# A hybrid decoder layer on one core: the mixing stage reordered, with the scan branch ahead of the attention

## What is computed

```
z = rmsnorm(x, g_mix) @ w_in
q, k, v, lru_x, lru_g, sc_b, sc_c, sc_u = split(z)
a = sliding_window_attention(q, k, v, sinks)          # window 128, 8 query heads, 2 KV heads
xc = causal_conv4(lru_x) + bias
r, i = sigmoid(xc @ wa + ba), sigmoid(xc @ wi + bi)   # block-diagonal, 4 blocks of 64
h = scan(exp(-8 r softplus(-lam)), sqrt(1 - a^2) * i * xc)
b = h * gelu(lru_g)
c = sc_b * causal_conv3(sc_c * sc_u)
x = x + concat(rmsnorm(a), rmsnorm(b), rmsnorm(c)) @ w_out
u, g = split(causal_conv3(rmsnorm(x, g_ffn) @ w_up))
x = x + (silu(g) * u) @ w_down
y = rmsnorm(x, g_final)
```

## Time and profile before

| | |
|---|---|
| runs | 1273.22, 1272.29, 1272.14 us |
| profiled execution | 1271.69 us, its span 1269.6 us |
| PE busy | 1173.3 us, 92% |
| DVE, ACT, POOL busy | 796.7, 337.4, 85.1 us |
| mean granted clock of TensorE | 0.963 |
| chain that ended last | PE 84%, DVE 9%, ACT 3%, POOL 1%, issue 1% |

### The profile page before, as it was taken

One profiled execution on the slowest core, in us unless ns is written; L12 is line 12 of the kernel. 1 busy time (PEld: TensorE's weight loads), 2 busy tenths in 40 slices (PEclk: granted clock), 3 DMA queues, 4 the chain that ended last, 5 costly groups with the idle time before them and its releaser, 6 DMA issues.

```text
span 1269.6 us, 18130 instructions
## 1 busy us (share of the span) xinstructions
PE 1173.3 (92%) x6972; PEld 1117.2 (88%) x6972; DVE 796.7 (63%) x1489; ACT 337.4 (27%) x512; POOL 85.1 (7%) x54
## 2 busy tenths in 40 slices
PE   7898899997587878999999999999999999999976
PEld 7897667677477878999999999999999999999965
DVE  6416456849765456756666666666666766666657
ACT  7112375544244233211111111111121211111132
POOL 0311000011023430000000000000000000000000
PEclk9998799999779888999999999999999999999988
DMA  6220000010323321111111111111111011111003
GB/s 221 88 78 21 17 17 17 17 35 34 119 100 100 116 92 59 34 52 48 50 50 49 34 50 50 50 33 50 49 50 50 33 50 50 50 50 42 24 14 134
DMA packets 25174, 72.11 MB, mean 57 GB/s; under 512 B 3472, under 2 KB 10000, under 8 KB 25104
## 3 DMA queue, kind: packets, MB, share of 16 engines
q1 hardware_dynamic: 21984, 64.44, 15.0%
q10 hardware_dynamic: 3152, 7.15, 1.6%
HBM read 66.76 MB, written 5.87 MB: 57 GB/s over the span
## 4 chain that ended last, share of the span: by engine, by line
PE 84%; DVE 9%; ACT 3%; POOL 1%; issue 1%; ACTq 0%; DMA 0%; DVEq 0%; SPq 0%
PE psum L1214 68%; PE psum L1371 6%; PE psum L1323 2%; PE psum L1246 2%; PE psum L1277 2%; POOL w_lo L385 1%; PE psum L1415 1%; PE psum L1333 1%; PE psum L1259 1%; ACT h_hi L1437 1%; ACT w_hi L424 1%; DVE zb L837 1%; PE psum L1269 1%; DVE att L818 1%; DVE zb L953 1%
## 5 line engine op out<-in xcount | busy, mean ns | idle before, releaser
L1214 PE MATMUL psum<-h_hi,w_hi 128*128 128x344 f32 x1392 | 455.3, 327 | 4.4 <-POOL w_lo L385 4.4
L1214 PE MATMUL psum<-h_lo,w_hi 128*128 128x344 f32 x1392 | 449.0, 323 | 0.0
L1214 PE MATMUL psum<-h_hi,w_lo 128*128 128x344 f32 x1392 | 448.7, 322 | 0.0
L1214 PEld LDWEIGHTS psum<-h_hi,w_hi 128*128 128x128 f32 x1392 | 265.4, 191 | 11.3 <-issue 5.7
L1214 PEld LDWEIGHTS psum<-h_lo,w_hi 128*128 128x128 f32 x1392 | 265.3, 191 | 1.4 <-issue 0.5
L1214 PEld LDWEIGHTS psum<-h_hi,w_lo 128*128 128x128 f32 x1392 | 265.4, 191 | 0.0
L424 ACT ACTIVATE w_hi<-raw 128x1024 fp32r<-128x1024 f32 x106 | 111.7, 1057 | 494.9 <-PE psum L1214 456.3
L1214 PE MATMUL psum<-act_hi,w_hi 128*128 128x344 f32 x528 | 175.1, 332 | 0.0
L1085 DVE TENSOR_TENSOR x_sb<-psum,x_sb 128x344 f32<-128x344 f32 x240 | 122.0, 515 | 83.6 <-PE psum L1214 83.6
L1214 PE MATMUL psum<-act_hi,w_lo 128*128 128x344 f32 x528 | 170.1, 322 | 0.0
L1214 PE MATMUL psum<-act_lo,w_hi 128*128 128x344 f32 x528 | 169.3, 321 | 0.0
(11 more groups left out here) (193 smaller groups left out, 1188.8 us busy)
## 6 DMA issues: line engine op xcount, KB each, us to landing
raw<-in_w SPq DMA_DIRECT2D x106, 512.0 KB, 3.2
x_sb<-in_x ACTq DMA_DIRECT2D x8, 516.0 KB, 5.0
out_y<-x_sb SPq DMA_DIRECT2D x12, 344.0 KB, 2.4
x_sb<-in_x SPq DMA_DIRECT2D x2, 1376.0 KB, 11.4
x_sb<-in_x SPq DMA_DIRECT2D x4, 344.0 KB, 5.4
zb<-in_ck ACTq DMA_DIRECT2D x1, 512.0 KB, 3.8
zb<-in_cv ACTq DMA_DIRECT2D x1, 512.0 KB, 4.5
out_k_old<-in_k_keep ACTq DMA_DIRECT2D x1, 508.0 KB, 4.8
```

The costliest lines, as they stand in the source:

```text
L1214: ins = mm(out, a, b, start=(at == 0), stop=(at == n - 1))
```

## The change

The slots are loaded in another order: k, lru_x, lru_g, lru_x, lru_g, v, q (4), sc_c, sc_u, sc_c, sc_u, sc_b, sc_b. The first 30 jobs (slots 0 to 9) run without attention, and under them the whole scan branch: convolutions, gates (three matmuls in a row into three banks), sigmoids, decays, scan, and the B norm.

The 16 attention steps then hold the 12 jobs of sc_c and sc_u, six chunks of 3 matmuls to a step, three before the tasks and three behind (`fill`). The six jobs of sc_b follow, two in the last two steps. Their eviction multiplies by the convolution, which was scaled by the norm before. The A norm of tile 0 is taken within the steps. The norms A and C of tiles 1 and 2, the scalings and splits of these tiles stand under output jobs 0 to 13, the split and squares of the new x by one or two blocks under jobs 8 and 14 to 23. The feed-forward part begins with six jobs (two slots, tile by tile, six PSUM banks), each waiting block by block for the split of x; the third tile is split under them. The issues of the small transfers go from ACT to SP, with the reload of x. The DVE twin of `x2_hi`, `x2_lo`, makes `h_lo` of each block and adds its squares to one sum.

```diff
+K_SLOT, LX_SLOTS, LG_SLOTS, V_SLOT, Q_SLOT0, SC_SLOTS, SU_SLOTS, SB_SLOT0 = 0, (1, 3), (2, 4), 5, 6, (10, 12), (11, 13), 14
+Z_BLOCK = (0, 6, 7, 8, 9, 1, 2, 3, 4, 5, 10, 11, 13, 14, 12, 15)
...
+FILL_JOB0 = NT * SC_SLOTS[0]
+SB_JOB0 = NT * SB_SLOT0
...
+FILLS = NT * 4 * KD // UNITS
+FILL_END = {(KD * (n + 1) - 1) // FILLS: n for n in range(NT * 4)}
+X2_AT = {8: (0, 0, 1), 14: (0, 1, 3), 15: (0, 3, 5), 16: (0, 5, 7), 17: (0, 7, 8), 18: (1, 0, 2), 20: (1, 2, 4), 21: (1, 4, 6),
+         22: (1, 6, 7), 23: (1, 7, 8)}
...
+    for t, j in enumerate((3, 5, 6)):
+        put(j, ("norm", "x", t), "A")
+    put(20, ("v", 0), "V")
...
+        put(25 + t, ("norm", "B", t), "A")
+    for i in range(UNITS + 2):
+        if i >= 2:
+            put(("step", i), ("pv", i - 2), "V")
+        if i < 4:
+            put(("step", i), ("sample", i), "V")
+        if i == 10:
+            put(("step", i), ("norm", "A", 0), "A")
+    put(SB_JOB0 + 2, ("norm", "C", 0), "A")
+    for o, name in ((1, "A1"), (3, "C1"), (8, "A2"), (10, "C2"), (18, "X0")):
+        put(OUT_JOB0 + o, ("norm", name[0], int(name[1])), "A")
+    put(FFN_JOB0, ("norm", "X", 1), "A")
+    put(FFN_JOB0 + 3, ("norm", "X", 2), "A")
...
+                if s == 4:
+                    sp.wait_ge(gate_zeroed, 1)
...
+                if s == 9:
+                    sp.wait_ge(job_read, NT * (V_SLOT + 1))
...
+                if s == 10:
+                    sp.wait_ge(b_ready, 2)
...
+                if s == OUT_SLOT0 + 2:
+                    sp.wait_ge(scratch_free, 1)
...
             root(("norm", "x", 1), rstd[:, tile(1)], D)
+            hi(3)
             root(("norm", "x", 2), rstd[:, tile(2)], D)
...
+            hi(4)
+            sigmoids(0, 0)
+            hi(5)
+            sigmoids(0, 1)
+            decays(0)
+            lru_sqrt(0)
+            gelu(0)
+            hi(6)
+            hi(7)
+            sigmoids(1, 0)
+            sigmoids(1, 1)
+            decays(1)
+            lru_sqrt(1)
+            hi(8)
+            gelu(1)
+            act.wait_ge(b_ready, 2)
+            square(zb[:, 6:8, :], sq_b)
+            hi(9)
+            for t in range(NT):
+                root(("norm", "B", t), rstd_b[:, tile(t)], 2 * P)
+            hi(10)
...
+                if i % 4 == 0:
+                    hi(11 + i // 4)
+                if i == 8:
+                    act.wait_ge(att_ready, 6)
+                    square(q_sb[:, :, tile(0)], sq_a0)
...
+            def x2_hi(t, k0, k1):
+                if k0 == 0:
+                    act.wait_ge(job_done, OUT_JOB0 + KD * (t + 1))
+                    if t:
+                        act.wait_ge(task_done, done_at(("norm", "X", t - 1)))
+                for k in range(k0, k1):
+                    act.wait_ge(job_read, OUT_JOB0 + KD * t + k + 1)
+                    nc.scalar.activation(h_hi[:, k, tile(t)], x_sb[:, k, tile(t)], ACT.Copy,
+                                         scale=gain_ffn[:, k:k + 1]).then_inc(x2_hi_ready, 1)
+                    if k > 2:
+                        act.wait_ge(x2_added, (KD - 1) * t + k - 2)
+                    nc.scalar.activation(x2_sq[k % 2] if k else x2_sum, x_sb[:, k, tile(t)],
+                                         ACT.Square).then_inc(x2_sq_ready, 1)
...
             merged_ab(0)
+            square_c(0)
+            root(("norm", "C", 0), rstd_c[0], 2 * P)
             merged_c(0)
+            hi(OUT_SLOT0)
+            for o in range(NT * KD):
+                hi(OUT_SLOT0 + o + 1)
+                if o in (0, 6):
+                    square_a(1 + o // 6)
+                if o in (1, 7):
+                    square_c(1 + o // 6)
+                if o in (1, 8):
+                    root(("norm", "A", 1 + o // 8), rstd_a[1 + o // 8], HG * P)
+                if o in (3, 10):
+                    root(("norm", "C", 1 + o // 10), rstd_c[1 + o // 10], 2 * P)
+                if o in (4, 11):
+                    merged_ab(1 + o // 11)
+                if o in (5, 12):
+                    merged_c(1 + o // 12)
+                if o in X2_AT:
+                    x2_hi(*X2_AT[o])
+                if o == 18:
+                    root(("norm", "X", 0), rstd[:, tile(0)], D)
+            hi(FFN_SLOT0 + 1)
+            root(("norm", "X", 1), rstd[:, tile(1)], D)
+            x2_hi(2, 0, KD)
+            root(("norm", "X", 2), rstd[:, tile(2)], D)
...
+                if s in LX_SLOTS:
                     if t == 0:
+                        dve.wait_ge(xc_ready, 1)
                         V.memset(x_pad[:, 0:3], 0.0)
                     evac(j, x_pad[:, 3:], samples(x_pad, 4)[:, :, 3])
...
+                elif s in LG_SLOTS:
+                    evac(j, g_in[LG_SLOTS.index(s)])
+                elif s == V_SLOT:
+                    evac(j, vT)
+                else:
+                    evac(j, q_sb[:, s - Q_SLOT0, :])
+                if j in (7, 15):
+                    conv_lru((j - 7) // 8)
+                if j in (12, 19):
+                    gate_input((j - 12) // 7)
+                if j in (13, 20):
+                    lru_root((j - 13) // 7)
+                if j in (14, 21):
+                    lru_scan((j - 14) // 7)
...
+            for i in range(UNITS + 2):
+                if 1 <= i <= UNITS:
+                    rescale(i - 1)
+                if i < UNITS:
+                    score_max(i)
+                if i == 8:
+                    sc_conv(0)
+                if i == UNITS:
+                    sc_conv(1)
+                if i >= 2:
                     att_evac(i - 2)
...
+                if i < 4:
+                    sample_task(i)
+                if i in FILL_END:
+                    fill_evac(FILL_END[i])
+                if i == 9:
+                    sq_tree("A", 0, HG, sq_a0)
+                if i == 12:
+                    a_scale(0)
+                if i >= UNITS:
+                    sb_evac(i - UNITS)
...
+            for o in range(NT * KD):
+                if o + 1 < NT * KD:
+                    w_lo2(OUT_SLOT0 + o + 1)
                 else:
                     dve.wait_ge(w_lo_ready, FFN_SLOT0)
                     w_lo_ffn(FFN_SLOT0)
...
+                out_evac(o)
+                if o in (0, 7):
+                    sq_tree("A", 1 + o // 7, HG, sq_a)
+                if o in (2, 9):
+                    a_scale(1 + o // 9)
+                    sq_tree("C", 1 + o // 9, 2, sq_c)
+                if o in (4, 11):
+                    c_scale(1 + o // 11)
+                if o in (5, 6, 12, 13):
+                    t, k0 = 1 + o // 12, 3 * (o in (6, 13))
+                    ab_lo(t, k0, k0 + 3)
+                    if k0:
+                        c_lo(t)
+                if o in X2_AT:
+                    x2_lo(*X2_AT[o])
+                if o == 19:
+                    reciprocal(("norm", "X", 0), rstd[:, tile(0)])
+            w_lo_ffn(FFN_SLOT0 + 1)
...
-            w_lo_ffn(FFN_SLOT0 + 1)
+            x2_lo(2, 0, KD)
+            reciprocal(("norm", "X", 1), rstd[:, tile(1)])
             carry_in(0, pad_g)
-            ffn_evac(FFN_JOB0, 0, pad_g, None)
-            ffn_evac(FFN_JOB0 + 1, 1, pad_g, None)
-            reciprocal(("norm", "X", 2), rstd[:, tile(2)])
-            ffn_evac(FFN_JOB0 + 2, 2, pad_g, None)
+            carry_in(1, pad_u)
+            for f in range(len(FIRST_JOBS)):
+                s, t = FIRST_JOBS[f]
+                if f == 4:
+                    reciprocal(("norm", "X", 2), rstd[:, tile(2)])
+                ffn_evac(FFN_JOB0 + f, t, (pad_g, pad_u)[s], None, first_ps[f])
             gate_half(0)
             w_lo_ffn(FFN_SLOT0 + 2)
-            carry_in(1, pad_u)
-            for t in range(NT):
-                ffn_evac(FFN_JOB0 + 3 + t, t, pad_u, None)
+            dve.wait_ge(conv_g_ready, 1)
             up_half(0)
...
+            def fill(i, lo, hi):
+                for chunk in range(FILLS * i + lo, FILLS * i + hi):
+                    n, k = divmod(chunk, KD)
+                    j = FILL_JOB0 + n
+                    s, t = z_job(j)
+                    if k == 0:
+                        w_lo_wait(s, None)
+                        pe.wait_ge(job_read, j - 2)
+                    wh, wl = wslot(s, k)
+                    mm(job_ps[j % 3], wh, h_hi[:, k, tile(t)], start=(k == 0), stop=False)
+                    mm(job_ps[j % 3], wh, h_lo[:, k, tile(t)], start=False, stop=False)
+                    ins = mm(job_ps[j % 3], wl, h_hi[:, k, tile(t)], start=False, stop=(k == KD - 1))
+                    if k == KD - 1:
+                        ins.then_inc(job_done, 1)
...
+            for j in range(FILL_JOB0):
+                if j < len(FIRST_JOBS):
+                    first_job(j, 0, h_ready).then_inc(job_done, 1)
+                else:
+                    job(j, *z_job(j)).then_inc(job_done, 1)
+                if j in (10, 11, 17, 18):
+                    gates(j // 16, (10, 11, 17, 18).index(j) % 2)
+                if j == 20:
```

(28 more changed lines are left out.)

540 lines of the change are left out of this document (235 added, 305 removed).

## The result

Measured together on one chip, the changed kernel takes 1213.01 us (median of four runs, 1211.76 to 1214.87) and the kernel before 1272.22: a ratio of 0.9539, 95% interval 0.9528 to 0.9551. The forecast was 1203, in a range of 1190 to 1222.

The account below looks back on a forecast made before the run. PE was taken as the bound, with gains only from its waits and slow matmuls before 508.4 us. Stretches summed to 439.5 + 761.2 = 1200.7, plus 2.1 around: 1203 on the median's scale, range 1190 to 1222.

Parts of the forecast that it names:

- First 30 jobs: Start to attention: 21 jobs after 46.8 us, plus gates, norms and transposes; ACT's work at nothing; attention from 137 us.
- held by ACT or the scan: Rival, first 30 jobs: six weight slots each 1.5 us late, late scan stops jobs; 12 more, 1215; chance 0.15.
- Attention steps: 16 steps: 8.0 us each in steps 4 to 15, 38.8 for steps 0 to 3, 3.4 exposed on DVE; 138.2 us.
- Last two steps and B jobs: Between attention steps and output projection: six jobs, two products, transposes, a norm and a weight wait; 28 us.
- Output projection: 24 jobs 90.5 us, five norms 2.9, queue waits 5.9, POOL and DVE interference 5.4; 104.7 us in all.
- The term for POOL and DVE: Output jobs from 14 on: POOL halves delay DVE, jobs take 4.3 to 4.4 us, 0.6 shows nine times; 5.4 us.
- The queue waits: Output projection: PE's bare waits from ACT's and DVE's queues, for a norm, held-up weights and a root; 5.9 us.
- Entry of the feed-forward part: First six feed-forward jobs: 5.5 us wait for DVE's weight 2 split, 1.6 for slow matmuls; 31 us, nothing gained.
- output part becomes DVE's: Rival, output projection: late jobs also wait for ACT's squares and POOL, 5.5 us each; 18 more, 1221; chance 0.17.
- slower: Rival, attention steps: overlap of two units lost, 12.8 us a step in series; 77 more, 1280; chance 0.02.
- no effect: Rival, whole kernel: the waits of PE come back elsewhere one for one; chance 0.01.
- Nearly all waits go: Rival: no 5.5 us feed-forward stall, steps at PE's bare 7.84, half the output waits gone; 1189; chance 0.12.

Follow-up runs that it names:

- number 3: Changed kernel with the second channel's gate matmuls put after jobs 18 and 19 instead of 17 and 18 on PE: 1207.51 us.
- number 9: Changed kernel with feed-forward weight 2's split and the attention root earlier, second gates later, and ACT's weight 3 split behind the third input-norm root: 1191.96 us.
- number 7: Kernel before with only ACT's split of weight 3 moved ahead of the third root of the input norm: 1265.11 us, ratio 0.9950.
- number 4: Changed kernel with POOL's part of each output weight split cut from 512 to 8 columns, the rest not computed: 1207.88 us.
- number 1: Changed kernel with DVE's split of feed-forward weight 2 moved from behind the gate convolution to behind the fifth eviction: 1206.62 us.

## Why the forecast held, and where its 10 us went

- **First 30 jobs, 6.8 us short of the 137.6 that the terms add up to: the step that failed.** I had worked out what POOL and DVE cost each other for the late output jobs alone, and put it at nothing in the first 30 jobs. I had put "1.5 us late" on the second convolution and nothing on ACT and the input norm. The wait for the convolution is 4.2 us, 2.7 more, and by the rows above two DVE instructions held by POOL's splits account for all 4.2 (2.30 us for 0.14 and 2.31 for 0.23), so that the order behind the scan alone would have cost nothing; number 3 covers this wait and does not test its cause. Its gates and the job behind it run slowly, about 1.7 (2.29 and 4.96 us from start to start, against 1.48 and 4.04). The job ahead of the input norm of tile 2 waits 0.4 for an eviction, and that norm 1.4, which is POOL's split of weight 3 beside DVE's addition (0.52 us of work, 2.57 long). That is 6.2 of 6.8. With numbers 3 and 9 applied the attention starts at 137.35. The bare count (21 jobs, 15 single matmuls, transposes) was right and the cover of the rest was not: the earlier weight 3, which I had costed as pure gain (number 7: 5.9 of 6.2), moved a POOL instruction beside one of DVE's. ACT's long block, which the rival "held by ACT or the scan" rested on, cost nothing; its other half, a late DVE stopping the gates in PE's queue, came true with about half of its 12 us.
- **Attention steps, 1.9 short, out of two errors.** Quiet steps take 7.88 us (8.0), steps 0 to 3 36.4 (38.8), the convolution and the norm's additions 2.0 (3.4): 5.2 us better. One step then takes 15.2 instead of 7.9, for the root. I had asked what DVE and ACT have in a step by durations, not where in ACT's queue the root stands and which PSUM tile it holds.
- **Last two steps and B jobs:** 28.6 for 28.
- **Output projection:** 104.8 for 104.7. The agreement to 0.1 us is partly luck. The late jobs take 4.25 us on the mean, but this holds a norm (0.6) and a wait of 1.4 for POOL's half, which the forecast counted apart or not at all; without them it is 4.05, not 4.3 to 4.4. The term for POOL and DVE was 5.4, all of it in the late jobs; number 4 measures 3.6 there and 1.4 before them, 4.9 together. The queue waits (5.9) are what number 4 leaves above the jobs and norms: 99.9 - 93.4 = 6.5. The two errors cancel. The mechanism was right: a split takes 0.57 us alone and 1.62 beside a POOL half. The rule of the Trainium skill (SBUF — State Buffer, "Who interferes with whom"), on which the prediction drew, is borne out for these DVE instructions. One row was misread: the POOL half of 1.31 us in the earlier trace rows does not lie alone, it starts 0.3 us into four DVE splits, which take 2.89 us.
- **Entry of the feed-forward part:** 29.6 and a slow job behind it, 2.4 in the rest; I had 31 with 1.6 for the slow job in it, so 32.0 against 31. "Nothing gained" there was right, and number 1 shows the reason.
- **Rest:** 761.2 as soon as that wait is gone. A slip of reading that nothing hangs on: the lowest clock in the earlier trace rows is 0.89, not 0.88.
- The rivals "output part becomes DVE's", "slower" and "no effect" fell with these numbers. "Nearly all waits go" (1189) was wrong for this kernel, and close to what the moved pieces give, 1192, though by another way: it had the output waits halve and the 5.5 us go, not the holds of the first 30 jobs.

## What to carry to other kernels

When a reordering is costed, look up for each moved instruction not only how long it takes but what it stands behind, which buffer it holds for someone else, and which engine's instruction comes to lie beside it: the three waits that were left cost 18 us, and each went with a move of one or two lines. Judge such moves by the length of their own stretch; a stretch in which the clock falls for varying times moves a median by as much as the edit does. Interference between two engines that is priced in one stretch has to be looked for in every stretch where both work. Taking work from the engine that bounds a stretch need not give back the time of that work: its waits grow, and its clock can fall.

## What the hardware showed that I had not expected

- How long a short DVE instruction can be held: 128x8 took 2.31 us (0.23 in the first convolution), another 128x8 2.30 (0.14 in the second scan), and 128x344 2.57 us (0.52 in number 9). The first ends with POOL's split at 90.3, the second with the one before at 81.1, and the third, 37.63 to 40.20, outlasts POOL's (37.28 to 39.83) by little. It is the POOL instruction's length that counts, not that of DVE's own. In number 7 the same addition ends at 37.66, just ahead of POOL's start at 37.70, and takes 0.52 us.
- Less work on PE went with a lower clock: with two thirds of the fill matmuls left out, the granted clock of 144 to 192 us was 0.68 (0.89 in the changed kernel), and of the 27 us expected 5 came.
- The same code, up to a given point, met the lower of the two clocks (1.2 of 2.4 GHz) for stretches of different length in different executions: 44.3 to 49.2 us for the same five steps.
